# Combining the experts' rows by diagonal products on TensorE, and the second combining stage joined to the block behind it

## The chip, the cores and the metric

The kernel runs on one core of one Trainium2 chip. TensorE (PE) multiplies, VectorE (DVE), ScalarE (ACT) and GpSimd (POOL) do the elementwise work, and SyncE (SP) issues nearly all DMAs. The metric is the device time of one execution in microseconds (us), as the median of several.

## The reference, cut to what matters

512 tokens of width 1024 go through a first block of two layers and then a second block of two layers, all in fp32. In the first block each layer is a mixer (windowed attention, then latent attention), a layer norm, a routed expert stage and a second layer norm:

```
h = layer_norm(alpha * h + mixer(h), ln_g[i, 0], ln_b[i, 0])
y = hier_moe(h, ...)        # each token: the sum of 2 of 32 experts, each times a weight
h = layer_norm(alpha * h + y, ln_g[i, 1], ln_b[i, 1])
```

The second block has no experts: in each layer `x + rms_norm(mixer(rms_norm(x)))` and the same around a gated feed-forward. Its mixer joins a 31-tap convolution, stick-breaking attention, retention and a short convolution.

## The kernel before

The residual `k.resid` stays in SBUF as four tiles of 128 tokens x 1024. The expert stage (`experts`) leaves `alpha * h` in it and each token's two expert rows, not yet weighted, in a DRAM tensor `y_dram`; the two weights of a token lie in SBUF (`weight[:, c, t]`). What comes behind it is called an opening here. There are two.

**First opening**, at the head of `latent_layer`. SP loads the rows of a tile (1 MB each, line 1394), gains and weight pieces. VectorE's `weigh(t)` adds the two weighted rows to the residual (lines 1783 and 1784, one pass each) and takes the statistics (430, 432); ScalarE makes the inverse root (`AfterMix.root`, 437 and 439); VectorE's `norm` does two passes (447, 450). TensorE transposes the tile (`turn_x`, 1448), ScalarE copies the transposed tile out of PSUM rounded to fp32r (`split_high`, 1628), and VectorE subtracts that copy to get the low part (`split_low`, 1790). Every product with a weight is three fp32r products of high and low parts (`split_matmul`, 226 to 228), so weights are split as well: `high(p)` on ScalarE (1646) and `low(p)` on VectorE (1799), which frees the `raw` buffer for the next load. Each engine's order is written out by hand at the end of its function: VectorE does `weigh` 0, 1, `norm` 0, `weigh` 2, `norm` 1, `low(0)`, and so on. TensorE begins `down_tile` with tiles 0 and 1 (the first half of the columns) and takes tiles 2 and 3 once they are split.

**Second opening**, `combine` and the head of `second_block`. `combine` is a stage of its own: VectorE sums, takes statistics and normalizes all four tiles (1255 to 1270), ScalarE takes square roots (1285), GpSimd clears the semaphores of retired stages. A stage ends with a barrier of all engines, `close` adds another one with 12 more clears. Then `second_block` starts: SP loads the first two weight pieces, a gain and 22 small parameter rows; TensorE transposes the parameters (2381), ScalarE keeps them (2623). The RMS norm of a tile is ScalarE's square with a sum (2445), VectorE's scale-and-add-epsilon (2661), ScalarE's root (2432), VectorE's reciprocal and pass (2663, 2674). Then transpose (2092), high (2450) and low (2678) parts as above. `in_halves` runs four units on tiles 0 and 1, turning tile 3 behind its third, and then four on tiles 2 and 3. The same `finish`/`root`/`inverse_root` serve every norm of the block.

**Mixer of the second block** (`mixer` in each engine's function, once a layer). TensorE alternates projections (`project(u)`, 24 products of 512 columns) with attention and retention. Near its end: `ret_last(1)` makes scores, `decayed(1, 2)` on VectorE (2724) weights them, `ret_mix(1)` (2196) multiplies them with the values; `project(24)`, the statistics product (2279), which waits for the convolution's 62 taps (2701). VectorE's order there is `taps(6)`, `decayed(1, 0)`, `decayed(1, 1)`, `low(l, 11)`, `decayed(1, 2)`, `taps(8)`, `low(l, 12)`.

Of the kernel before, what the change touches and what calls it, by code (L numbers as in the profile page):

```python
# [20 lines left out]
P = 128  # L21
SEQ = 512
D = 1024
# [96 lines left out]
class Stage:  # L120
# [12 lines left out]
    def close(self):  # L133
        with self.nc.Block() as block:
            @block.gpsimd
            def _(pool):
                for s in self.sems:
                    pool.sem_clear(s)
        self.ctx.close()
        self.sem_ctx.close()  # L140

# [29 lines left out]
class Core:  # L171
# [16 lines left out]
    def clear_stale(self, eng):  # L188

        for st in self.stale:  # L190
            for s in st.sems:
                eng.sem_clear(s)

# [207 lines left out]
class AfterMix:  # L401
# [25 lines left out]
    def stats_of(self, k, dve, t):  # L427

        for half in range(2):
            dve.bn_stats(self.stats[:, t, half, :], k.resid[:, t, half * 512:(half + 1) * 512]).then_inc(self.counted, 1)  # L430
        dve.wait_ge(self.counted, 2 * t + 2)
        dve.bn_aggr(self.mv[:, t, :], self.stats[:, t, :, :]).then_inc(self.var_ready, 1)
# [8 lines left out]
    def norm(self, k, dve, t):  # L441

        x = k.resid[:, t, :]
# [3 lines left out]
        dve.scalar_tensor_tensor(x, x, self.mv[:, t, 0:1], self.gain[:, :], ALU.subtract, ALU.mult).then_inc(self.gained, 1)  # L447
# [4 lines left out]
    def turn(self, k, pe, rt, t):  # L452
# [4 lines left out]
        for j in range(ND):  # L457
            ins = pe.transpose(k.ps[:, 4 + j // 4, (j % 4) * P:(j % 4 + 1) * P], k.resid[:, t, j * P:(j + 1) * P], k.ident)
            if j % 4 == 3:
                ins.then_inc(rt.turned, 1)  # L460

# [763 lines left out]
def combine(k, layer, r):  # L1225

    st = Stage(k.nc, f"comb{layer}")
    gain, shift, warm = st.sb("gain", [P, D]), st.sb("shift", [P, D]), st.sb("warm", [P, 1])
    stats, mv, sd, rs = st.sb("stats", [P, NT, 2, 6]), st.sb("mv", [P, NT, 2]), st.sb("sd", [P, NT]), st.sb("rs", [P, NT])
    y_in = [st.sem(f"y{i}") for i in range(NT)]  # L1230
    gain_in, var_ready, sd_ready, summed, counted, gained, shifted, chain = (
        st.sem(n) for n in ("gain_in", "var", "sd", "summed", "counted", "gained", "shifted", "chain"))
    rows = k.ring[:, 0:4, :].rearrange("p s (c d) -> p s c d", c=2)
    y_rows = r.y_dram.rearrange("(c t p h) d -> t p c (h d)", c=TOPK, p=P, h=2)
    with k.nc.Block() as block:
        @block.sync
        def _(sp):
            for t in range(NT):
                sp.dma_start(rows[:, t], y_rows[t]).then_inc(y_in[t], 16)
                if t == 0:  # L1240
                    sp.dma_start(gain[:, :], k.a["ln_g"][layer, 1:2, :].to_broadcast([P, D])).then_inc(gain_in, 16)
                    sp.dma_start(shift[:, :], k.a["ln_b"][layer, 1:2, :].to_broadcast([P, D])).then_inc(gain_in, 16)

        @block.gpsimd
        def _(pool):
            k.clear_stale(pool)

        @block.vector
        def _(dve):
            link = Link(dve, chain)  # L1250

            def weigh(t):
                x = k.resid[:, t, :]
                dve.wait_ge(y_in[t], 16)
                link(dve.scalar_tensor_tensor(x, rows[:, t, 0, :], r.weight[:, 0, t:t + 1], x, ALU.mult, ALU.add))
                dve.scalar_tensor_tensor(x, rows[:, t, 1, :], r.weight[:, 1, t:t + 1], x, ALU.mult, ALU.add).then_inc(summed, 1)
                dve.wait_ge(summed, t + 1)
                for h in range(2):
                    dve.bn_stats(stats[:, t, h, :], x[:, h * 512:(h + 1) * 512]).then_inc(counted, 1)
                dve.wait_ge(counted, 2 * t + 2)  # L1260
                link(dve.bn_aggr(mv[:, t, :], stats[:, t, :, :]))
                dve.tensor_scalar(sd[:, t:t + 1], mv[:, t, 1:2], LN_EPS, None, ALU.add).then_inc(var_ready, 1)

            def finish(t):
                x = k.resid[:, t, :]
                dve.wait_ge(sd_ready, t + 1)
                dve.scalar_tensor_tensor(x, x, mv[:, t, 0:1], gain[:, :], ALU.subtract, ALU.mult).then_inc(gained, 1)
                link(dve.reciprocal(rs[:, t:t + 1], sd[:, t:t + 1]))
                dve.wait_ge(gained, t + 1)
                dve.scalar_tensor_tensor(x, x, rs[:, t:t + 1], shift[:, :], ALU.mult, ALU.add).then_inc(shifted, 1)  # L1270

            weigh(0)
            dve.wait_ge(gain_in, 32)
            for t in range(NT):
                if t + 1 < NT:
                    weigh(t + 1)
                finish(t)
            dve.wait_ge(shifted, NT)

        @block.scalar  # L1280
        def _(act):
            act.activation(warm[:, :], k.cst[:, C_ONE:C_ONE + 1], ACT.Sqrt)
            for t in range(NT):
                act.wait_ge(var_ready, t + 1)
                act.activation(sd[:, t:t + 1], sd[:, t:t + 1], ACT.Sqrt).then_inc(sd_ready, 1)
    k.free_stale()
    st.close()


LAT_UNITS = [(n, g) for n in range(NT) for g in range(4)]  # L1290

# [1613 lines left out]
```

## Time and profile before

| what | before |
| --- | --- |
| median of 3 runs (lowest, highest) | 2867.61 us (2865.9, 2874.51) |
| the profiled execution, its span | 2867.99 us, 2866.2 us |
| PE, PEld busy | 2492.6 us (87%), 1851.9 us (65%) |
| DVE, ACT, POOL busy | 1104.7 us (39%), 768.2 us (27%), 159.5 us (6%) |
| mean granted TensorE clock | 0.942 |
| 754 to 802: first opening | PE transposes from 772.0, products from 789.69 |
| 1576.7 to 1651: second opening | combining until 1610.8, products from 1636.57 |

The span runs from the first to the last instruction, and all starts are counted from its beginning. PE is the matmuls, PEld the weight loads beside them. An fp32 product counts as two instructions, an fp32r product as one. "Idle before <- releaser" is how long the engine stood still ahead of a group, and what ended that. The granted clock is a share of full speed: 1.00 is 2.4 GHz, 0.50 is 1.2 GHz.

### The profile page before, as it was taken

The numbers are of one execution on the slowest core, as the hardware profiler recorded it, in microseconds if no ns is written. First come the engines' busy times: TensorE is split into PE (matmuls) and PEld (weight loads), VectorE is DVE, ScalarE is ACT, GpSimd is POOL, SyncE is SP. The second block draws the span as 40 slices with busy tenths as digits, with TensorE's granted clock in tenths as the row PEclk, the third lists the DMA queues.
The fourth block names the chain that finished last, engine by engine and source line by source line (L and its number), as shares of the span: only waits on it lengthen the run. The fifth ranks groups of instructions, "written<-read, shape, count | busy, mean of one in ns | idle before, by whom it ended". The sixth has DMA issues, their size and how long they took to land. (4 is left out here: it accounts for less than half of the span.)

```text
span 2866.2 us, 36705 instructions
## 1 busy us (share of the span) xinstructions
PE 2492.6 (87%) x14450; PEld 1851.9 (65%) x14450; DVE 1104.7 (39%) x1653; ACT 768.2 (27%) x1219; POOL 159.5 (6%) x279
## 2 busy tenths in 40 slices
PE   8895998878388968987887299999999999999998
PEld 7574565544266655654544287688888876888887
DVE  3754111000444551110000565655551565655632
ACT  2430110000134510101000243444341452533331
POOL 0000111111000001111111000000000000000000
PEclk9997999999798979999999599999999999999999
DMA  5228999999612078999997421312332222223331
GB/s 153 59 81 330 407 405 409 411 408 402 218 70 74 8 285 342 405 404 406 408 409 291 143 96 59 118 59 88 103 118 102 82 68 80 74 89 102 98 123 52
DMA packets 174814, 576.38 MB, mean 201 GB/s; under 512 B 20496, under 2 KB 104016, under 8 KB 125042
## 3 DMA queue, kind: packets, MB, share of 16 engines
q1 hardware_dynamic: 164146, 558.07, 51.3%
q0 software_dynamic: 10560, 16.81, 1.8%
q8 instruction: 76, 1.25, 0.2%
q14 instruction: 32, 0.26, 0.0%
HBM read 569.56 MB, written 23.07 MB: 207 GB/s over the span
## 5 line engine op out<-in xcount | busy, mean ns | idle before, releaser
L1158 PE MATMUL ps<-first_weights,moe_xsT 128*64 128x256 f32 x2688 | 312.8, 381 | 50.1 <-DMA first_weights<-in_moe_w_up 32.1
L226 PE MATMUL ps<-l_h_hi,l_w_hi 128*128 128x512 f32 x896 | 353.1, 394 | 0.0
L227 PE MATMUL ps<-l_h_lo,l_w_hi 128*128 128x512 f32 x896 | 349.0, 389 | 0.0
L228 PE MATMUL ps<-l_h_hi,l_w_lo 128*128 128x512 f32 x896 | 349.0, 389 | 0.0
L1214 DVE TENSOR_TENSOR moe_hid<-moe_silu,ps 128x256 f32<-128x256 f32 x64 | 26.9, 421 | 796.2 <-PE ps L1158 796.2
L1158 PEld LDWEIGHTS ps<-first_weights,moe_xsT 128*64 128x64 f32 x2688 | 223.8, 137 | 148.8 <-issue 99.6
L2656 DVE TENSOR_TENSOR l_w_lo<-l_raw,l_w_hi 128x2048 fp32r<-128x2048 f32 x76 | 174.0, 2291 | 293.2 <-ACT l_w_hi L2427 293.2
L1195 ACT ACTIVATE moe_ys<-ps 128x512 f32<-128x512 f32 x64 | 38.2, 597 | 687.2 <-PE ps L1176 687.2
L1176 PE MATMUL ps<-first_weights,moe_hidT 128*64 128x512 f32 x672 | 178.9, 680 | 38.6 <-DVE moe_hidT L1216 38.6
L2427 ACT ACTIVATE l_w_hi<-l_raw 128x2048 fp32r<-128x2048 f32 x76 | 145.2, 1914 | 187.1 <-PE ps L228 176.0
L226 PEld LDWEIGHTS ps<-l_h_hi,l_w_hi 128*128 128x128 f32 x896 | 168.4, 188 | 37.7 <-issue 3.0
L1158 PE MATMUL ps<-first_ring,moe_xsT 128*64 128x256 f32 x1408 | 168.6, 391 | 26.3 <-DMA first_ring<-in_moe_w_up 14.0
L227 PEld LDWEIGHTS ps<-l_h_lo,l_w_hi 128*128 128x128 f32 x896 | 168.4, 188 | 35.4 <-issue 1.4
L228 PEld LDWEIGHTS ps<-l_h_hi,l_w_lo 128*128 128x128 f32 x896 | 168.3, 188 | 35.4
L1158 PEld LDWEIGHTS ps<-first_ring,moe_xsT 128*64 128x64 f32 x1408 | 119.6, 141 | 79.4 <-issue 52.8
L1176 PEld LDWEIGHTS ps<-first_weights,moe_hidT 128*64 128x64 f32 x672 | 60.6, 153 | 127.9 <-issue 127.9
L1176 PE MATMUL ps<-first_ring,moe_hidT 128*64 128x512 f32 x352 | 88.9, 650 | 20.1 <-DVE moe_hidT L1216 20.1
L1142 PEld LDWEIGHTS ps<-cst,moe_xs 64*128 64x128 f32 x528 | 68.9, 215 | 45.9 <-issue 24.6
L1142 PE MATMUL ps<-cst,moe_xs 64*128 64x64 f32 x528 | 78.0, 289 | 20.8 <-DMA moe_xs<-r_x,moe_take 20.8
L1130 POOL DMA_INDIRECT r_y<-moe_ys,moe_put x64 | 65.4, 1022 | 298.6 <-ACT moe_ys L1195 298.6
L2701 DVE SCALAR_TENSOR_TENSOR l_gate<-l_glu,l_par,l_gate 128x512 f32<-128x512 f32 x120 | 81.0, 744 | 0.1
L1192 ACT ACTIVATE moe_silu<-ps 128x256 f32<-128x256 f32 x64 | 24.5, 383 | 204.8 <-PE ps L1158 204.8
(545 smaller groups left out, 4279.6 us busy)
## 6 DMA issues: line engine op xcount, KB each, us to landing
first_weights<-in_moe_w_up SPq DMA_DIRECT2D x84, 1024.0 KB, 29.0
first_weights<-in_moe_w_down SPq DMA_DIRECT2D x84, 1024.0 KB, 28.8
first_weights<-in_moe_w_gate SPq DMA_DIRECT2D x84, 1024.0 KB, 28.3
first_ring<-in_moe_w_gate SPq DMA_DIRECT2D x44, 1024.0 KB, 28.1
first_ring<-in_moe_w_up SPq DMA_DIRECT2D x44, 1024.0 KB, 29.1
first_ring<-in_moe_w_down SPq DMA_DIRECT2D x44, 1024.0 KB, 28.9
l_raw<-in_ffn_up SPq DMA_DIRECT2D x44, 1024.0 KB, 5.1
l_raw<-in_w_in SPq DMA_DIRECT2D x24, 1024.0 KB, 5.3
```

The source lines that it names most:

```text
L226: pe.matmul(out, stationary[0], moving[0], start=first, stop=False)
L227: pe.matmul(out, stationary[0], moving[1], start=False, stop=False)
L228: return pe.matmul(out, stationary[1], moving[0], start=False, stop=last)
L1130: pool.indirect_dma_start(out=r.y_dram, out_offset=bass.IndirectOffsetOnAxis(ap=put[:, 0:1], axis=0), in_=ys[:, :], in_offset=None, bounds ...
L1142: ins = pe.transpose(k.ps[:, 0, j * SLOTS:(j + 1) * SLOTS], row_of_tile[:, j // 4, j % 4, :], k.cst[0:SLOTS, C_ID:C_ID + SLOTS])
L1158: ins = pe.matmul(k.ps[64 * h:64 * h + 64, 2 + m, 0:256], xsT[:, j, :], weights.gate_up[s][m][:, j, 256 * h:256 * h + 256], start=j == 0, ...
L1176: ins = pe.matmul(k.ps[64 * h:64 * h + 64, 4, :], hidT[:, j % 2, 64 * (j // 2):64 * (j // 2) + 64], weights.down[s][:, j, 512 * h:512 * h ...
L1195: act.activation(ys[:, :], k.ps[:, 4, :], ACT.Copy).then_inc(ys_kept, 1)
L1214: dve.tensor_tensor(hid[:, :], silu[:, :], k.ps[:, 3, 0:256], ALU.mult).then_inc(hid_kept, 1)
L2427: act.activation(ring[n][0], raw[:, m % 2, :], ACT.Copy).then_inc(hi_made, 1)
L2656: dve.tensor_tensor(lo, raw[:, m % 2, :], hi.bitcast(F32), ALU.subtract).then_inc(lo_made, 1)
L2701: ins = dve.scalar_tensor_tensor(acc, glu[:, i, c:c + SEQ], par[:, l, 2, 2 * c + i:2 * c + i + 1], acc, ALU.mult, ALU.add)
```

## The change

Both openings sum on TensorE. A new class `Collect` loads the rows, makes for each tile and choice a 128x128 diagonal matrix of the weights on ScalarE, and adds in PSUM: identity x residual, then diagonal x rows, all in fp32. A tile takes two banks, so the four tiles fill all eight. Statistics and the first normalizing pass read PSUM.

```
+    def diagonals(self, k, act):
+        for t in range(NT):
+            for c in range(TOPK):
+                ins = act.activation(self.diag[:, c, t, :], k.ident, ACT.Copy, scale=self.before.weight[:, c, t:t + 1])
+        ins.then_inc(self.spread, 1)
+
+    def own(self, k, pe):
+        for t in range(NT):
+            for half in range(2):
+                pe.matmul(k.ps[:, 2 * t + half, :], k.ident, k.resid[:, t, half * 512:(half + 1) * 512], start=True, stop=False)
+
+    def add(self, k, pe, t):
+        pe.wait_ge(self.spread, 1)
+        pe.wait_ge(self.y_in[t], 16)
+        for half in range(2):
+            for c in range(TOPK):
+                ins = pe.matmul(k.ps[:, 2 * t + half, :], self.diag[:, c, t, :], self.rows[t][:, c, half * 512:(half + 1) * 512], start=False, stop=c == TOPK - 1)
+        ins.then_inc(self.collected, 1)
```

`norm` is cut in two: `centre(k, dve, t, src)` does subtract mean and times gain from `src` (PSUM) into the residual, and `finish` does the second pass.

First opening, per engine:

```
 TensorE
+            cl.own(k, pe)
+            cl.add(k, pe, 0)
+            cl.add(k, pe, 1)
             turn_x(0)
+            cl.add(k, pe, 2)
             turn_x(1)
+            cl.add(k, pe, 3)
 GpSimd, behind its clears
+            for p in range(2):
+                pool.wait_ge(hi_made, p + 1)
+                pool.tensor_tensor(whole(p, 1), raw[:, p, :], whole(p, 0).bitcast(F32), ALU.subtract).then_inc(lo_made, 1)
 ScalarE
+            cl.diagonals(k, act)
             cm.root(act, 0)
             high(0)
             cm.root(act, 1)
             split_high(0)
+            high(1)
+            split_high(1)
             cm.root(act, 2)
-            split_high(1)
-            high(1)
+            split_high(2)
             cm.root(act, 3)
-            split_high(2)
             split_high(3)
 VectorE (weigh, norm, low(0) and low(1) go)
+            stats(0)                       # waits for collected, statistics from PSUM
+            cm.centre(k, dve, 0, tile_banks(0))
+            cm.finish(k, dve, 0)
+            stats(1)
+            cm.centre(k, dve, 1, tile_banks(1))
+            cm.finish(k, dve, 1)
             split_low(0)
+            stats(2)
+            cm.centre(k, dve, 2, tile_banks(2))
             split_low(1)
+            cm.finish(k, dve, 2)
+            stats(3)
+            cm.centre(k, dve, 3, tile_banks(3))
             split_low(2)
+            cm.finish(k, dve, 3)
             split_low(3)
+            dve.wait_ge(lo_made, 2)
```

Second opening: `combine` and `close` go. `second_block` begins with one short block, `sweep`, in which SP issues the loads of rows and gains while GpSimd, VectorE and ScalarE clear a third of the old semaphores each; its barrier stands ahead of the rest.

```
 TensorE
+            cl.own(k, pe)
+            for t in range(NT):
+                cl.add(k, pe, t)
             turn(opening, 0)
             turn(opening, 1)
-            turn(opening, 2)
-            pe.wait_ge(par_kept, 2)
             for l in range(DEPTH):
-                in_halves(l, ...)          # turned tile 3 behind its third unit
+                in_halves(l, ...)          # l == 0: tile 2 behind the second unit, tile 3 behind the fourth
+                if l == 0:
+                    turn_parameters()
 ScalarE
+            cl.diagonals(k, act)
+            deviation(0)                   # Sqrt of the variance + epsilon
+            finish(opening, 0, None)       # square with sum, root
+            deviation(1)
+            split_high(opening, 0)
+            finish(opening, 1, None)
             high(0, 0)
+            deviation(2)
+            split_high(opening, 1)
             high(0, 1)
             finish(opening, 2, None)
+            deviation(3)
+            split_high(opening, 2)
             finish(opening, 3, None)
             split_high(opening, 3)
 VectorE (normed: reciprocal and cm.finish; finish: the RMS norm's pass; stats: statistics and centre)
+            stats(0)
+            normed(0)
+            stats(1)
+            finish(opening, 0)
+            normed(1)
+            split_low(opening, 0)
+            stats(2)
+            finish(opening, 1)
+            split_low(opening, 1)
+            normed(2)
+            stats(3)
+            finish(opening, 2)
+            split_low(opening, 2)
+            normed(3)
+            finish(opening, 3)
+            split_low(opening, 3)
+            dve.wait_ge(lo_made, 2)
```

GpSimd makes the low parts of the first two weight pieces here too. The parameters are kept by ScalarE behind `high(l, 3)` in layer 0; TensorE waits for that ahead of `project(6)`, VectorE ahead of the taps, and the load of the rotation tables waits for the parameters' transposes.

In every norm of the second block the scale and epsilon move into ScalarE's root, and VectorE's instruction goes; ScalarE's `finish` of tile t waits for tile t-2's sum where there is no transpose:

```
-                act.wait_ge(g.biased, v)
-                act.activation(sd[...], sd[...], ACT.Sqrt).then_inc(g.rooted, 1)
+                act.wait_ge(g.squared, v)
+                act.activation(sd[...], ss[...], ACT.Sqrt, scale=1.0 / D, bias=eps[:, 0:1]).then_inc(g.rooted, 1)
```

In the mixer's VectorE order, in both layers:

```
                 decayed(1, 0)
                 decayed(1, 1)
+                decayed(1, 2)
                 low(l, 11)
-                decayed(1, 2)
                 taps(8)
```

## Rows read from the trace of the kernel before

**Rows 1.** The expert rows' tile and DMA issues, first opening
```profile
L1394 SPq DMA_DIRECT2D lat_rows<-r_y x4: 388/607/3402, 753.9 to 760.0; - x4
...
DMA to landing us min/median/max: 4.9/11.6/14.2
...
lat_raw<-in_b_w_down SPq DMA_DIRECT2D x2, 1024.0 KB, 14.1
```

**Rows 2.** Table by stretches: start:end length, busy time (instructions) of each engine, clock, DMA
```profile
772.00:789.60 17.60, 3.93 (x16) 3.13 (x16) 17.18 (x18) 4.84 (x7) 0.00 (x0) 0.50 0.45 111
789.60:794.50 4.90, 4.81 (x22) 4.81 (x23) 4.71 (x4) 0.00 (x0) 0.00 (x0) 0.50 0.02 3
1576.70:1612.60 35.90, 0.00 (x0) 0.00 (x0) 26.90 (x36) 2.30 (x6) 0.00 (x0) 0.50 0.38 147
1636.50:1641.00 4.50, 4.50 (x23) 4.50 (x23) 2.53 (x3) 1.02 (x1) 0.00 (x0) 0.50 0.00 0
1799.30:1803.80 4.50, 4.50 (x17) 1.75 (x17) 4.50 (x8) 0.00 (x0) 0.00 (x0) 0.50 0.00 0
```

**Rows 3.** Timeline, first opening: start, us, engine, line, operation, count [idle before]
```profile
768.18 1.91 ACT L1646 ACTIVATE lat_d_hi<-lat_raw 128x2048 fp32r<-128x2048 f32 x1 [4.54 <-DMA lat_raw<-in_b_w_down]
...
774.00 1.02 ACT L1628 ACTIVATE lat_x_hi<-ps 128x1024 fp32r<-128x1024 f32 x1 [3.49 <-PE ps L1448]
...
780.68 1.22 DVE L1790 TENSOR_TENSOR lat_x_lo<-ps,lat_x_hi 128x1024 fp32r<-128x1024 f32 x1
...
789.69 0.58 PE L226 MATMUL ps<-lat_x_hi,lat_d_hi 128*128 128x256 f32 x1 [9.11 <-DVE lat_x_lo L1790]
...
794.80 1.03 PE L1448 MATMUL ps<-cst,resid 128*128 128x128 f32 x8
...
801.95 0.38 PE L226 MATMUL ps<-lat_x_hi,lat_d_hi 128*128 128x256 f32 x1 [2.37 <-DVE lat_x_lo L1790]
```

**Rows 4.** Timeline, second opening
```profile
1578.15 1.78 SPq L1239 DMA_DIRECT2D first_ring<-r_y  x3
...
1584.20 1.29 DVE L1259 BATCH_NORM_STATS2 comb_stats<-resid 128x6 f32<-128x512 f32 x2
...
1609.55 1.28 DVE L1270 SCALAR_TENSOR_TENSOR resid<-resid,comb_rs,comb_shift 128x1024 f32<-128x1024 f32 x1
...
1612.66 1.00 SPq L2036 DMA_DIRECT2D l_raw<-in_w_in  x2
...
1624.51 1.04 ACT L2445 ACTIVATE l_end_xn<-resid 128x1024 f32<-128x1024 f32 x1
...
1636.57 0.56 PE L226 MATMUL ps<-l_h_hi,l_first_hi 128*128 128x256 f32 x1
...
1648.05 0.36 PE L226 MATMUL ps<-l_h_hi,l_first_hi 128*128 128x256 f32 x1
```

**Rows 5.** Timeline, end of the mixer in layer 0; last row: layer 1
```profile
1793.89 1.91 ACT L2427 ACTIVATE l_w_hi<-l_raw 128x2048 fp32r<-128x2048 f32 x1 [6.31 <-PE ps L228]
...
1795.83 2.29 DVE L2656 TENSOR_TENSOR l_w_lo<-l_raw,l_w_hi 128x2048 fp32r<-128x2048 f32 x1 [7.70 <-ACT l_w_hi L2427]
...
1799.10 5.38 DVE L2701 SCALAR_TENSOR_TENSOR l_gate<-l_glu,l_par,l_gate 128x512 f32<-128x512 f32 x8
...
1799.24 4.53 PE L2196 MATMUL ps<-l_wr,l_vt 128*64 128x512 f32 x16 [5.39 <-DVE l_wr L2724]
...
1809.81 1.88 PE L2279 MATMUL ps<-l_gate,cst 128*128 128x512 f32 x4
...
2425.16 1.88 PE L2279 MATMUL ps<-l_gate,cst 128*128 128x512 f32 x4
```

**Rows 6.** fp32 products (timeline) and a VectorE pass reading PSUM (its tile)
```profile
1705.21 4.50 PE L2187 MATMUL ps<-l_ln,cst 128*128 128x512 f32 x20
...
L2669 DVE SCALAR_TENSOR_TENSOR l_end_xn<-ps,l_rs,l_end_gain x8: 1282/1284/1286, 2227.4 to 2860.6; 128x1024 f32<-128x1024 f32 x8
```

**Rows 7.** Timeline, end of layer 0: the instruction ahead of a root
```profile
2231.27 0.15 DVE L2661 TENSOR_SCALAR l_sd<-l_ss 128x1 f32<-128x1 f32 x1 [1.29 <-ACT l_end_xn L2445]
```

More of the change, by code:

```diff
@@ L192, in clear_stale, with sweep, _ @@
                 eng.sem_clear(s)
+    def sweep(self, loads):
+        sems = [s for st in self.stale for s in st.sems]
+        third = -(-len(sems) // 3)
+        with self.nc.Block() as block:
+            @block.sync
+            def _(sp):
+                loads(sp)
+            @block.gpsimd
+            def _(pool):
+                for s in sems[:third]:
+                    pool.sem_clear(s)
+            @block.vector
+            def _(dve):
+                for s in sems[third:2 * third]:
+                    dve.sem_clear(s)
+            @block.scalar
+            def _(act):
+                for s in sems[2 * third:]:
+                    act.sem_clear(s)
+        self.free_stale()
     def free_stale(self):
@@ L441, in norm, with centre @@
     def norm(self, k, dve, t):
-        x = k.resid[:, t, :]
+        self.centre(k, dve, t, k.resid[:, t, :])
+        self.finish(k, dve, t)
+    def centre(self, k, dve, t, src):
         if t == 0:
@@ L1222, in experts @@
     st.retire(k)
[L1225 to L1287, printed above, removed]
@@ L1778, in _, with stats @@
             link = Link(dve, chain)
[L1780 to L1786 removed]
+            def stats(t):
+                dve.wait_ge(cl.collected, t + 1)
+                cm.stats_of_sum(k, dve, t)
             def split_low(t):
@@ L1988, in second_block, with first_loads @@
     rows = plan.put("rows", 32, [P, DEPTH, 3, P])
+    cl = Collect(st, plan, (36, 44, 68, 76), 24, before)
+    cm = AfterMix(st, plan, "c", 0, 84)
+    def first_loads(sp):
+        cl.load(sp, 0)
+        cm.load_gains(k, sp, DEPTH - 1, 1)
+        for t in range(1, NT):
+            cl.load(sp, t)
+    k.sweep(first_loads)
     in_w = [(w.hi[:, n, :], w.lo[:, n, :]) for n in range(2)]
@@ L2116, in up_unit, with in_halves @@
                 return ins
-            def in_halves(l, g, one, piece, made):
+            def in_halves(l, g, one, piece, made, turns=((), (), (3,), ())):
                 pe.wait_ge(g.h_lo, 2)
@@ L2124, in in_halves @@
                     one(q, slice(0, 2 * P))
-                    if q == 2:
-                        turn(g, 3)
+                    for t in turns[q]:
+                        turn(g, t)
                 pe.wait_ge(g.h_lo, NT)
```

153 lines of the change are left out of this document (74 added, 79 removed).

## The prediction

> **What bounds the kernel now.** I read the page first: TensorE is busy most of the span and the chain of waits runs through it. So I looked in the table by stretches for those where TensorE stands still, and in the timeline for what it waits for there. Three places matter.
>
> First opening: the second layer's block starts at 753.9 (the first load of expert rows) [rows 1]. VectorE combines, normalizes and splits four tiles, busy 17.18 of 17.60 us, while TensorE's granted clock is 0.50, its lower level (1.2 GHz) [rows 2]. TensorE's first product starts at 789.69, the second half of the tokens at 801.95 [rows 3].
>
> Second opening: the combining block takes 1576.7 to 1612.6, with no TensorE instruction [rows 2]; the second block starts its loads at 1612.66, its first product runs at 1636.57. The last quarter of the first two tiles' work starts at 1648.05 [rows 4] and has 24 products; at the upper clock they take some 0.12 us each, about half of the 4.81 us that 22 of this shape take at the lower [rows 2]. So the second half of the tokens begins at 1650.9.
>
> Mixer, once in each layer: TensorE stands 5.39 us before the last retention product because VectorE does a 2.29 us low part before the last decay products; that low part itself had waited 7.70 us for ScalarE, idle [rows 5]. The ScalarE copy it waited for starts at 1793.89, when TensorE's preceding projection ends. The product then takes 4.53 us [rows 5], at a granted clock of 0.50 [rows 2], so after idling it runs at half the upper clock, 2.3 us lost.
>
> Elsewhere in the second block TensorE is hardly ever idle, so what these places give stays given: weights, copies and low parts are all released by products or by each other, none by the clock on the wall.
>
> **Prices of what is added.** TensorE gets 24 fp32 products of 128x512 in each opening (8 own, 16 weighted). The nearest row holds ten fp32 products, 2560 columns in all, in 4.50 us [rows 6]; less 0.17 for the last one's drain that is 1.69 ns a column, 0.87 us for 512. At 1.2 GHz it is 1.74. Two sustained stretches turn to 2.4 GHz after 4.9 and 4.5 us [rows 2], so a run that begins cold costs 2.25 us more: own takes 8 x 0.87 + 2.25 = 9.2 us, each tile's add 3.5 us. Eight diagonals on ScalarE are 1024 columns, the width of a 1.04 us square [rows 4]; with seven more starts an estimated 2.5 us, hidden behind own. VectorE loses two weighted adds of 1.28 a tile and keeps statistics (1.29 + 0.21) and two passes of 1.28; that centre now reads PSUM is free, since the same operation from PSUM takes 1.284 [rows 6]. Transpose of a tile: 1.03 at 2.4 GHz, twice that at 1.2; high part 1.02, low part 1.22 [rows 3].
>
> GpSimd gets two subtractions of 128x2048, which VectorE does in 2.29 [rows 5]. No row shows one on GpSimd. Low end 2.29; as high end I take four times that, 9.2; between them twice, 4.6, an estimate. The Trainium skill (GPSIMD Engine Reference, 3.1 Elementwise — side-by-side cycle accounting) gives 4497 ns against 2293 ns for this size; VectorE's row agrees with the second figure, no row here has the first, and with it the sum would be the same.
>
> **First opening.** Own runs from 753.9 to 763.2. The first expert tile lands 4.9 us after 753.9, the last no later than 14.2 after 760.0, at 774.2 [rows 1]. Adds end at 766.7 and 770.2. Tile 0: statistics to 768.3, centre 769.6, finish 770.9 (ScalarE's root lies beside centre); transposed to 772.1. Tile 1: statistics 772.4, centre 773.7, finish 775.0; add 2 has TensorE until 775.6, transposed to 776.7; add 3 to 780.2. The second weight piece is now copied before tile 1's high part. The two pieces have a median landing of 14.1 us [rows 1] and the first lands 12.2 after its issue at 756.0 (ScalarE starts on it at 768.18 [rows 3]), so the second, issued at 760.6, lands 16.0 later, 776.6; copy 778.5, high part 779.5, low part 780.8. First product at 780.9 against 789.69: 8.8 us. GpSimd's first subtraction (770.8 to 775.4) has 5.5 us to spare. Then 24 products at 2.4 GHz (2.9), transpose 784.9, high 786.0, low 787.2 (finish 2, statistics 3 and centre 3 lie before it, to 784.9), finish 3 788.5, transpose 789.6, high and low 791.8. Second half at 791.9 against 801.95: **10.0 us**. Before, the first half ran at 1.2 GHz; that is part of it.
>
> **Second opening.** The new block issues its loads in 3.2 us (the last three take 1.78 from 1578.15 [rows 4]); 17 clears on each of three engines stay under that, since 12 of them with all barriers fit between the last pass, 1610.8, and 1612.66. With 0.9 for barriers TensorE starts at 1580.8. Own to 1590.0, adds to 1593.5, 1597.0, 1600.5, 1603.9; the tiles have landed before each. VectorE: statistics 0 1595.1, centre 1596.4, finish 1597.9; tile 1 statistics and centre 1600.7; round 0 (ScalarE's square and root ended 1599.5) 1602.2; finish 1 1603.7. TensorE turns tile 0 at 1603.9 to 1604.9, high 1606.0, low 1607.3; statistics and centre 2 to 1610.1; round 1 to 1611.6; turned cold 1613.7, high 1614.8, low 1616.1. ScalarE's first weight copy ends 1609.4, GpSimd's subtraction 1614.0. First product at 1616.2 against 1636.57: 20.4 us. But then VectorE is late again: 48 products half cold, 7.7 us, to 1623.9; turn 2 1624.9, low 1627.2; finish 3 1628.7; square and root 1630.2; round 3 1631.7; turn 1632.7; low 1635.0. Second half at 1635.1 against 1650.9: 15.8. The parameter transposes now stand behind it, 0.9 us, and the tables' load behind them, with projections in front of its use: **14.9 us**.
>
> **Mixer.** The scores for the last decay products were long ready, since VectorE stood idle before 1795.83. Now they run there, and the last retention product starts at 1793.9 and takes half of 4.53, the projection 5.5 (in layer 0 it ended at 1809.81, 6.0 after the product, the first 0.6 at the low clock): 1801.7. What is late next is the convolution: low part to 1798.1, eight taps 5.38 [rows 5], to 1803.5. The statistics product starts then against 1809.81, 6.3 us. In layer 1 it starts at 2425.16, and the taps end 5.6 us before that. TensorE takes the lead again behind: VectorE's next low part moves forward with ScalarE's copy by more than that. Together **11.9 us**.
>
> **Roots.** One VectorE instruction of 0.15 us with its two hand-overs goes from each chain [rows 7]: 0.3 at the turn from layer 0 to 1, 0.3 at the last tile, 0.3 at the feed-forwards: **0.9 us**. The new wait on tile t-2's sum is met 8 us early.
>
> **Sum.** The profiled execution took 2867.99 us (span 2866.2, 1.8 around it), 0.4 above the median 2867.61. 2867.99 - 10.0 - 14.9 - 11.9 - 0.9 = 2830.3; against the median 2829.9. I forecast **2830**.
>
> **Rivals.**
> A: GpSimd's subtractions and VectorE's passes get in each other's way. As a mechanism here: a VectorE pass with both inputs in SBUF (finish, the rounds) that comes during a GpSimd subtraction waits for its end. Finish 1 at 773.7 waits to 775.4, finish 2 a little: 1.1 us by the second half. Round 1 at 1610.3 waits to 1614.0 and round 2 to the end of the second subtraction: second half 1638.6 instead of 1635.1, 3.5. Together 4.6: 2834.5. For it: both have work at once in both openings. Against: no row of before shows the two together. The Trainium skill (SBUF — State Buffer, Who interferes with whom) says just this: a VectorE instruction with two SBUF inputs contends with a GpSimd one that reads SBUF, and the later one blocks fully; no run yet shows it.
> B: GpSimd needs 9.2 us. Its end passes the first opening's start (780.0) not at all and the second's (1618.6 for 1616.2; the second piece later by 4): some 4 us, with A's waits up to 12: 2834 to 2842.
> C: the moved decay products give nothing, the chain behind (taps, low parts, ScalarE's copies) being the bound: 2867.6 - 25.8 = 2842. For it: 1.8 us of the idle time is already convolution. Against: that chain is released by ScalarE's copy behind the projection, which moves forward by more than the statistics product does.
> D, the other side: the clock. If fp32 products with their gaps don't bring TensorE up and it stays at 1.2 GHz through both openings, 24 products cost 41.8 us. First opening: adds and two turns end at 799.6, second half at 816.2 against 801.95 and runs 4.5 longer: 18.7 lost. Second: adds to 1622.6, first product 1635.8, second half 1662.6 against 1650.9 and 9 longer, 0.9 and as much again for parameters: 22.5 lost. With the other terms kept, 2867.6 + 41.2 - 12.8 = 2896. It decides once about two thirds of the products run cold. For it: 0.50 throughout the openings, and fp32 products at 1.2 GHz in 1799.24's row. Against: those came after idling, and both sustained starts rose within 5 us.
>
> **Chances.** Forecast 0.50, A 0.28, B 0.07, C 0.10, D 0.03, something else 0.02. Quicker barriers and hand-overs can give some 6 us more, and the mixer what the convolution holds back, 1.8 in each layer: 2821. C with A ends at 2846: range 2821 to 2846. This measurement tells 0.3% (8.6 us) from no change: faster 0.95, same 0.02, slower 0.03.
>
> **What would show it.** First product 28 us after the first row load instead of 35.8, and about 40 us after the second's instead of 59.8; granted clock 1.00 from about 5 us into own; 0.87 us a product; the 5.39 us waits gone and some 1.8 us before the statistics product; GpSimd's subtractions near 4.6 us, and VectorE passes of 1.28 us grown long beside them if A holds. Wrong would be an opening that ends with TensorE's adds instead of VectorE, or a mixer as long as before.

## The result, and the profile after

The changed kernel takes 2843.64 us (median of 4 runs, 2842.8 to 2846.85) against 2868.07 of the kernel before on the same chip (4 runs): the ratio is 0.9913, 95% interval 0.9896 to 0.9931. The forecast was 2830, the range 2821 to 2846. The gain is 24.4 us where 38 were forecast, so the time lies inside the range, but 13.6 us of the gain are missing, and the rest of the study is about them.

The head of the page and the granted clock row of the changed kernel:

```profile
span 2841.4 us, 36857 instructions
PE 2533.8 (89%) x14546; PEld 1870.4 (66%) x14546; DVE 1078.5 (38%) x1597; ACT 776.1 (27%) x1234; POOL 179.0 (6%) x284
PEclk9996999999998978999999799999999999999999
```

TensorE is busy 41 us longer than before, in the main by its added products (48 of about 0.86 us), in a span that is 25 us shorter; GpSimd has 20 us more, its four subtractions.

First opening, the changed kernel's timeline (start, us, engine, line, operation, count, idle before). The rows answer to [rows 3]; the first load of expert rows stands at 755.17, 1.3 us later than before with nothing changed ahead of it (over all traces of this study it stands between 752.85 and 755.76).

```profile
755.21 9.28 PE L512 MATMUL ps<-resid,cst 128*128 128x512 f32 x16 [10.13 <-PEq L1148]
...
772.08 4.60 POOL L1436 TENSOR_TENSOR lat_d_lo<-lat_raw,lat_d_hi 128x2048 fp32r<-128x2048 f32 x1 [16.74 <-ACT lat_d_hi L1646]
...
775.17 2.59 DVE L474 SCALAR_TENSOR_TENSOR resid<-resid,lat_crs,lat_cshift 128x1024 f32<-128x1024 f32 x1
...
779.59 4.56 POOL L1436 TENSOR_TENSOR lat_d_lo<-lat_raw,lat_d_hi 128x2048 fp32r<-128x2048 f32 x1 [2.92 <-ACT lat_d_hi L1646]
...
782.71 2.52 DVE L474 SCALAR_TENSOR_TENSOR resid<-resid,lat_crs,lat_cshift 128x1024 f32<-128x1024 f32 x1
782.84 0.39 PE L242 MATMUL ps<-lat_x_hi,lat_d_hi 128*128 128x256 f32 x1 [0.50 <-DVE lat_x_lo L1787]
...
801.35 0.34 SPq L1406 DMA_DIRECT2D lat_tables<-in_k_ropeb  x1
```

Own took 9.28 us (forecast 9.2) and the first product came 27.7 us after the first load (35.8 before, forecast gain 8.8, here 8.1). But two finishing passes of VectorE, 1.28 us elsewhere, took 2.59 and 2.52 us, each while GpSimd subtracted.

Second opening, same columns; it answers to [rows 4]:

```profile
1570.15 0.39 SPq L499 DMA_DIRECT2D l_rows<-r_y  x1
...
1602.53 4.49 POOL L2095 TENSOR_TENSOR l_first_lo<-l_raw,l_first_hi 128x2048 fp32r<-128x2048 f32 x1 [28.29 <-ACT l_first_hi L2452]
...
1603.35 4.76 DVE L2708 SCALAR_TENSOR_TENSOR l_end_xn<-resid,l_rs,l_end_gain 128x1024 f32<-128x1024 f32 x1
...
1608.16 1.97 PE L2109 MATMUL ps<-cst,l_end_xn 128*128 128x128 f32 x8 [10.01 <-DVE l_end_xn L2708]
...
1612.50 0.58 PE L242 MATMUL ps<-l_h_hi,l_first_hi 128*128 128x256 f32 x1 [2.37 <-DVE l_h_lo L2712]
...
1613.06 5.22 POOL L2095 TENSOR_TENSOR l_first_lo<-l_raw,l_first_hi 128x2048 fp32r<-128x2048 f32 x1 [6.04 <-ACT l_first_hi L2452]
...
1616.71 2.65 DVE L2708 SCALAR_TENSOR_TENSOR l_end_xn<-resid,l_rs,l_end_gain 128x1024 f32<-128x1024 f32 x1
...
1627.92 1.09 PE L2109 MATMUL ps<-cst,l_end_xn 128*128 128x128 f32 x8 [1.11 <-DVE l_end_xn L2708]
...
1631.38 0.58 PE L242 MATMUL ps<-l_h_hi,l_first_hi 128*128 128x256 f32 x1 [2.37 <-DVE l_h_lo L2712]
...
1646.45 0.35 SPq L2072 DMA_DIRECT2D l_tables<-in_k_roper  x1
```

The pass of 4.76 us began 0.8 us behind the subtraction and could only work once that ended at 1607.02; TensorE and ScalarE stood behind it. First product 42.4 us after the first load (59.8 before): 17.5 gained, 20.4 forecast.

The mixer came as forecast. The last retention product and the statistics product of layer 0, then the latter in layer 1 [rows 5]:

```profile
1777.69 2.37 PE L2213 MATMUL ps<-l_wr,l_vt 128*64 128x512 f32 x16
1787.44 1.98 PE L2299 MATMUL ps<-l_gate,cst 128*128 128x512 f32 x4 [1.72 <-DVEq L2820]
...
2398.63 1.98 PE L2299 MATMUL ps<-l_gate,cst 128*128 128x512 f32 x4 [1.72 <-DVEq L2820]
```

No wait before the product, 2.37 us instead of 4.53, and 1.72 us of waiting for the convolution behind it (forecast 1.8).

The granted clock of TensorE is the other finding. The changed kernel's table by stretches (start:end length, busy time (instructions) of PE, PEld, DVE, ACT and POOL, clock, DMA share, GB/s): the start of the second half of the tokens in both openings, then the beginning of the down projections of both layers.

```profile
793.90:799.00 5.10, 5.10 (x31) 5.10 (x32) 3.17 (x3) 1.31 (x2) 0.00 (x0) 0.68 0.01 2
1631.30:1636.30 5.00, 4.92 (x23) 4.92 (x24) 4.36 (x3) 2.37 (x2) 0.00 (x0) 0.50 0.01 3
2107.00:2113.00 6.00, 6.00 (x20) 4.72 (x20) 4.80 (x6) 4.83 (x4) 0.00 (x0) 0.72 0.13 55
2719.00:2725.00 6.00, 6.00 (x21) 4.74 (x21) 4.80 (x5) 4.32 (x4) 0.00 (x0) 0.73 0.08 9
```

and the same places of the kernel before:

```profile
802.00:807.00 5.00, 5.00 (x42) 5.00 (x43) 3.13 (x3) 1.27 (x2) 0.00 (x0) 1.00 0.00 0
1650.00:1655.00 5.00, 5.00 (x44) 5.00 (x43) 4.35 (x3) 4.84 (x4) 0.00 (x0) 1.00 0.00 0
2127.00:2133.00 6.00, 4.22 (x19) 3.49 (x19) 4.72 (x8) 3.51 (x4) 0.00 (x0) 1.00 0.50 172
2739.00:2751.00 12.00, 10.22 (x45) 8.11 (x44) 10.69 (x11) 5.87 (x6) 0.00 (x0) 1.00 0.26 89
```

Before, the waits in front of the first opening's second half (2.37 us) and of the down projections (1.78 us) cost only themselves, and in the second opening TensorE did not wait there at all. Now a wait stands in front of all four (2.37 us in each opening), and each is followed by a stretch at 1.2 GHz. A mean clock of 0.72 over 6 us is (1 - 0.72) x 6 = 1.7 us lost. The wait ahead of the down projection is the same to the hundredth in both kernels, first the kernel before, then the changed one:

```profile
2128.79 0.50 PE L226 MATMUL ps<-l_w_hi,l_act_hi 128*128 128x512 f32 x1 [1.78 <-DVE l_conv L2831]
```

```profile
2106.50 0.50 PE L242 MATMUL ps<-l_w_hi,l_act_hi 128*128 128x512 f32 x1 [1.78 <-DVE l_conv L2866]
```

### The profile page after: what moved, and what is told of

It is laid out like the page before. It is cut to its first block and busy times, and to the rows that moved or that the text cites. A ratio compares the mean times of both kernels' runs of the same rounds, so it can differ in the third digit from the quotient of the medians.

```text
span 2841.4 us, 36857 instructions
## 1 busy us (share of the span) xinstructions
PE 2533.8 (89%) x14546; PEld 1870.4 (66%) x14546; DVE 1078.5 (38%) x1597; ACT 776.1 (27%) x1234; POOL 179.0 (6%) x284
## 5 line engine op out<-in xcount | busy, mean ns | idle before, releaser
L242 PEld LDWEIGHTS ps<-l_h_hi,l_w_hi 128*128 128x128 f32 x896 | 168.2, 188 | 37.4 <-issue 2.9
L242 PE MATMUL ps<-l_w_hi,l_act_hi 128*128 128x512 f32 x192 | 77.0, 401 | 3.6 <-DVE l_conv L2866 3.6
```

The costliest lines, as they stand in the source:

```text
L242: pe.matmul(out, stationary[0], moving[0], start=first, stop=False)
```

## The experiments

Two theories came out of this reading. The **port theory** is rival A: a VectorE pass with both inputs in SBUF waits for GpSimd's subtraction, as if both needed one port of SBUF that only one of them can hold. "Port" and "lock" are names for this waiting; what the traces show is the waiting. The **clock theory**: short waits of TensorE that cost nothing before now cost the granted clock. Each expectation is on record as written before its run.

The openings are measured from the first load of expert rows to the issue of the rotation tables' load, which waits until TensorE has got a set way into the work behind the opening. That is one profiled execution for each kernel; time is the median, d the difference to the changed kernel.

```
kernel               time     d      ratio to before (95%)    1st    2nd opening
before               2868.07                                  54.1   86.0
changed              2843.64         0.9913 (0.9896, 0.9931)  46.2   76.3
e1_mixer             2858.17  +14.5  0.9969 (0.9958, 0.9980)
e2_no_subtraction    2839.11   -4.5  0.9903 (0.9887, 0.9918)  45.0   73.5
e3_fill              2838.82   -4.8  0.9901 (0.9886, 0.9917)  45.5   74.4
e4_order             2832.63  -11.0  0.9880 (0.9865, 0.9895)  46.9   66.0
e5_openings          2851.72   +8.1  0.9941 (0.9927, 0.9954)  46.9   77.4
e6_low_on_vector     2843.85   +0.2  0.9919 (0.9905, 0.9932)  48.6   75.6
e7_order_both        2829.25  -14.4  0.9862 (0.9846, 0.9877)  42.9   66.0
e8_order_fill        2826.18  -17.5  0.9860 (0.9845, 0.9876)  42.7   65.7
e9_fill_down         2838.80   -4.8  0.9902 (0.9885, 0.9920)  47.1   76.2
e10_subtract_twice   2845.43   +1.8  0.9922 (0.9906, 0.9937)  47.0   76.3
```

The kernel before took 2868.1, 2868.2 and 2867.2 beside the three groups of experiments, so the times can be set side by side within some 2 us; single runs of one kernel spread over 2 to 12. The changed kernel, e5, e9 and e10 have the same work on the path of both openings: their means, 46.8 and 76.5, are what the others are compared with below. These four spread over 0.9 and 1.2 us, so a difference in an opening of less than about 1 us says nothing.

**e1_mixer.** In the kernel before:

```
                 decayed(1, 1)
+                decayed(1, 2)
                 low(l, 11)
-                decayed(1, 2)
```

> The kernel before with one thing of the change: in the mixer VectorE does the last decay products ahead of its low part. My theory (TensorE leads, the freed 5.4 us wait and the cold product are worth 6.3 us in layer 0 and 5.6 in layer 1): 2867.8 - 11.9 = 2856, and the trace shows the last retention product with no wait before it and some 1.8 us of idle before the statistics product. Rival C (taps, low parts and copies are the bound behind it): 2867. Clock theory, from the trace of the changed kernel (short idle times of TensorE now and then cost the granted clock, with no rule that the change sets): up to 1.7 us may be lost again in each down projection, 2859; then the stretch behind the 1.8 us wait for the convolution shows a granted clock under 1.00.

2858.17 us, 10.0 under before. In place it is the forecast: the product takes 2.37 us with no wait, and 1.72 us of idle stand before the statistics product. In layer 0 the down projection keeps its clock, in layer 1 it doesn't:

```profile
2116.00:2128.00 12.00, 10.22 (x46) 8.13 (x45) 10.27 (x11) 6.38 (x7) 0.00 (x0) 1.00 0.24 87
2731.00:2737.00 6.00, 5.88 (x19) 4.70 (x20) 4.76 (x6) 4.84 (x4) 0.00 (x0) 0.72 0.26 104
```

11.7 us (6.2 and 5.5, as the changed kernel's trace has them) less one loss of 1.7 is the 10.0 measured; that they meet so closely is in part luck, since e1's runs spread over 3.9 us and only the profiled one shows its clock. Rival C is out.

**e2_no_subtraction.** In both openings of the changed kernel (the low parts are zeros that GpSimd wrote earlier, so that part of the product adds nothing):

```
-                pool.tensor_tensor(lo, raw[:, n, :], hi.bitcast(F32), ALU.subtract).then_inc(lo_made, 1)
+                pool.sem_inc(lo_made, 1)
```

> The changed kernel, with GpSimd's four subtractions left out (the low parts of the first two weight pieces of each of the two openings are zero, filled by GpSimd before; its hand-over to TensorE stays behind ScalarE's copy). Port theory (a VectorE pass with both inputs in SBUF waits for GpSimd's subtraction to end): the passes of 2.59, 2.52, 4.76 and 2.65 us fall to 1.28; first opening 1 to 2 us shorter, second 3 to 4: 2843.6 - 5 = 2838.6. Rival (those passes are long for another reason, as a late operand from ScalarE or the DMA writes into SBUF): they stay long, 2843.6. Second rival (what waits behind them is TensorE's clock, not VectorE): passes fall to 1.28, the time stays within 1 us.

2839.11 us, 4.5 faster. The pass that took 4.76 us in the changed kernel, in e2:

```profile
1601.69 1.28 DVE L2714 SCALAR_TENSOR_TENSOR l_end_xn<-resid,l_rs,l_end_gain 128x1024 f32<-128x1024 f32 x1
```

All four passes are at 1.28. The first opening is 1.8 us shorter, the second 3.1. The loads into SBUF are the same in e2, so they were not what held the passes. The port theory stands, with its size. With this loss gone the prediction's walk through the queues holds nearly to the us: counted from the first row load, its first products are at 27.0 and 39.5 us and its second halves at 38.0 and 58.4; e2 has them at 26.4 and 39.3, and at 37.4 and 58.3 (the changed kernel at 27.7 and 42.4, and at 38.7 and 61.2).

**e3_fill.** In the changed kernel; the first lines in both openings (bank 3 in the first, 4 in the second; there behind a wait for the third low part), the second in each down projection. Cut to the products and the wait that they precede:

```
+                for n in range(5):
+                    pe.matmul(k.ps[:, 4, 0:2 * P], k.ident, k.resid[:, 0, 0:2 * P], start=True, stop=True)
                 pe.wait_ge(g.h_lo, NT)
...
+                for n in range(4):
+                    pe.matmul(k.ps[:, 4, 0:2 * P], zeros[:, :], k.resid[:, 0, 0:2 * P], start=False, stop=False)
                 pe.wait_ge(x.convolved, 4 * STEPS)
```

> The changed kernel, with products added that nobody reads: five fp32 128x256 (0.43 us each) into a free bank while TensorE waits for the last low part of each opening, and four with a zero stationary before the wait for the convolution in each down projection. Clock theory (a wait of 1.8 to 2.4 us there drops the granted clock to 0.50 for 2 to 4 us): the second halves start at clock 1.00, 1.5 us gained in the first opening, 2.2 in the second, 1.7 in each down projection: 2843.6 - 7 = 2836.5. Rival (the clock falls whatever TensorE does there, or the fill delays the start by as much as it saves): 2843 to 2845.

2838.82 us, 4.8 faster with more instructions. The four places in e3's table by stretches:

```profile
792.00:800.00 8.00, 7.79 (x57) 7.18 (x56) 4.45 (x4) 3.65 (x4) 0.00 (x0) 1.00 0.01 3
1630.00:1638.00 8.00, 7.79 (x57) 7.18 (x56) 5.64 (x3) 4.63 (x3) 0.00 (x0) 1.00 0.00 0
2102.00:2114.00 12.00, 11.96 (x53) 9.65 (x53) 10.68 (x11) 4.84 (x4) 0.00 (x0) 1.00 0.30 100
2718.00:2726.00 8.00, 8.00 (x37) 6.64 (x36) 4.86 (x3) 3.26 (x2) 0.00 (x0) 1.00 0.39 134
```

1.00 in all four. The openings are 1.3 and 2.1 us shorter by the traces. With TensorE busy in the wait the clock stays up; the rival, that it falls whatever TensorE does there, is out. Idle time alone doesn't decide it, since the same waits cost no clock in the kernel before. The traces of the four places add up to 6.8 us, the times show 4.8.

**e9_fill_down.** Only the lines in the down projections.

> The changed kernel with only the down projections' fill: four fp32 128x256 products with a zero stationary before TensorE's wait for the convolution. Clock theory (in the changed kernel, though not in the kernel before, this wait of 1.8 us costs the granted clock, 1.7 us in each layer): both down projections run at 1.00, 2843.6 - 3.4 = 2840.2. Rival (the mixer moves forward and something else in that phase is late): 2843 to 2845 and the clock, if it stays up, gives nothing.

2838.80 us: 4.8 faster, more than the 3.4 expected and as much as e3 with all four; the runs of each spread over 6 to 8 us, so e3 and e9 can't be told apart by their times. What the fills in the openings are worth is therefore shown by e3's trace alone, and not by a time. e9's down projections:

```profile
2102.00:2110.00 8.00, 7.96 (x36) 6.35 (x35) 6.68 (x9) 4.61 (x4) 0.00 (x0) 1.00 0.41 131
2714.00:2722.00 8.00, 7.96 (x36) 6.28 (x35) 6.72 (x8) 4.85 (x4) 0.00 (x0) 1.00 0.31 123
```

**e5_openings.** The changed kernel with the mixer's order of before (e1's diff, reversed).

> The changed kernel with the mixer's order of before (VectorE's low part ahead of the last decay products): what the two openings and the roots are worth by themselves. If the parts add up, the 10.0 us that the mixer gave alone are lost again: 2843.6 + 10 = 2853.6, that is 14 to 15 us under before. Rival (the parts hinder each other; the openings alone give the 24.9 us of the prediction, and the mixer's shift costs them later): 2843 to 2847.

2851.72 us, 8.1 slower: the mixer's move is worth 8.1 us on top of the openings, not 11.7 (e5's runs spread over 7.6 us). e5 has the cold retention product again, and its down projections keep their clock with no fill:

```profile
1784.35 4.36 PE L2213 MATMUL ps<-l_wr,l_vt 128*64 128x512 f32 x16 [5.38 <-DVE l_wr L2758]
```

```profile
2107.00:2122.00 15.00, 13.22 (x59) 10.61 (x58) 12.18 (x11) 6.92 (x7) 0.00 (x0) 1.00 0.31 98
2728.00:2740.00 12.00, 12.00 (x53) 9.95 (x54) 7.01 (x6) 6.03 (x5) 0.00 (x0) 1.00 0.52 192
```

11.7 - 2 x 1.7 = 8.3. The expectation's first figure was 1.9 too high. That fits its taking e1's 10.0, in which only one down projection lost its clock, though 1.9 us is also no more than two such times can differ by. Over all traces, one profiled execution of each kernel: with the mixer's product cold, at 1.2 GHz (before, e5), none of 4 down projections lost its clock; with it at 2.4 GHz and no fill (changed, e1, e2, e4, e6, e7, e10) 13 of 14 did; with the fill (e3, e8, e9) none of 6. That the one decides the other is a count, not a mechanism. Nothing near the wait tells the cases apart: in the traces of before, changed, e1, e5 and e10 TensorE is busy without a gap at clock 1.00 for 28 us ahead of it, and the wait is 1.78 us each time. Why a stretch 330 us earlier should matter stays open.

**e6_low_on_vector.** The changed kernel without GpSimd's subtractions; VectorE has `low(0)` and `low(1)` behind the finishing pass of tile 1 and the low part of tile 1 (first opening), `low(0, 0)` behind statistics and centre 2 and `low(0, 1)` behind the low part of tile 1 (second).

> The changed kernel with GpSimd's four subtractions given back to VectorE (2.29 us each, as VectorE's low parts before), right behind the high parts. Port theory: first opening 4.6 longer for VectorE less the 1.3 and 1.2 us of waits that go, some 2 us; second opening 2.3 in place of a wait of 3.5 and 2.3 in place of one of 1.4, about nothing: 2843.6 + 2 = 2845.6, so that moving them off VectorE was worth next to nothing. Rival (GpSimd takes them off the path for what they cost on VectorE): 4.6 in each opening, 2852.8.

2843.85 us, the same as the changed kernel. First opening 1.8 longer, second 0.9 shorter. As placed in the change, moving 9.2 us of VectorE's work to GpSimd was worth nothing that these runs can tell, since VectorE then waited 7.4 us in its four long passes.

**e10_subtract_twice.** GpSimd subtracts the first piece of the second opening twice.

```
+                if n == 0:
+                    pool.tensor_tensor(lo, raw[:, n, :], hi.bitcast(F32), ALU.subtract).then_inc(cleared, 1)
+                    pool.wait_ge(cleared, 3)
                 pool.tensor_tensor(lo, raw[:, n, :], hi.bitcast(F32), ALU.subtract).then_inc(lo_made, 1)
```

> The changed kernel with GpSimd's subtraction of the first weight piece of the second opening done twice in a row (the same result, 4.5 us more for GpSimd). If the port is held over both: VectorE's pass of 4.76 us grows to 9.2 and the opening by 4.5, 2848. If the port changes hands between two instructions: VectorE's pass slips in at the end of the first, 4.76 as before, the second subtraction starts 1.1 to 1.3 later, ends about where the first product starts, and costs 0.2 to 1 us: 2844.3. Without a lock (only the piece's landing counts): the second subtraction ends 0.9 us before the first product, nothing, 2843.6, and VectorE's pass is what it was or overlaps the second.

2845.43 us, 1.8 above the changed kernel and inside its spread; the second opening is unchanged, 76.3. The time alone decides little. The second theory of the three is what the trace has:

```profile
1601.58 4.49 POOL L2096 TENSOR_TENSOR l_first_lo<-l_raw,l_first_hi 128x2048 fp32r<-128x2048 f32 x1 [28.34 <-ACT l_first_hi L2455]
1602.39 4.76 DVE L2711 SCALAR_TENSOR_TENSOR l_end_xn<-resid,l_rs,l_end_gain 128x1024 f32<-128x1024 f32 x1
1606.15 5.38 POOL L2098 TENSOR_TENSOR l_first_lo<-l_raw,l_first_hi 128x2048 fp32r<-128x2048 f32 x1
1607.21 1.97 PE L2112 MATMUL ps<-cst,l_end_xn 128*128 128x128 f32 x8 [10.01 <-DVE l_end_xn L2711]
```

VectorE works between the two, and the second subtraction waits for VectorE in turn: 5.38 instead of 4.49. It ends at 1611.53, and the first product follows at 1611.68, as that theory had it. So the waiting is by instruction and goes both ways.

**e4_order.** The changed kernel, the same instructions in another order. The second opening (VectorE, then ScalarE, then TensorE's `turns`; cut: ScalarE's `high(0, 1)` and its deviations 2 and 3 also come earlier):

```
             stats(1)
+            stats(2)
             finish(opening, 0)
             normed(1)
             split_low(opening, 0)
-            stats(2)
             finish(opening, 1)
+            stats(3)
             split_low(opening, 1)
             normed(2)
-            stats(3)
-            finish(opening, 2)
-            split_low(opening, 2)
             normed(3)
+            finish(opening, 2)
             finish(opening, 3)
+            split_low(opening, 2)
...
             deviation(0)
+            high(0, 0)
             finish(opening, 0, None)
...
-  ((), (2,), (), (3,))
+  ((2,), (3,), (), ())
```

In the first, `split_low(0)` stands ahead of finish 1, and statistics and centre 3 ahead of finish 2 and 3.

> The changed kernel with another order of the same instructions in the openings: VectorE's statistics and centre passes (one input in PSUM) stand where GpSimd subtracts, ScalarE makes the high part of the first weight piece of the second opening some 8 us earlier, and TensorE turns tiles 2 and 3 of the second opening after its first and second quarter instead of second and fourth. Port theory with the order of waits read from the trace: passes of 1.28 us throughout; second opening: first product about 5 us earlier, second half 7.7 us earlier (53.5 us after the first row load instead of 61.2) and without a cold restart (2); first opening 1.5 to 3 us: 2843.6 - 11.5 = 2832. Rival (what binds is TensorE's cold product train and the landing of the weights, the lock hides behind them): under 3 us, 2841.

2832.63 us, 11.0 faster. The second opening is 10.5 us shorter, the first not at all, where 1.5 to 3 were expected (VectorE waited there for ScalarE's fourth root, as e7's expectation says). e4's timeline beside GpSimd's first subtraction of the second opening:

```profile
1592.43 4.53 POOL L2095 TENSOR_TENSOR l_first_lo<-l_raw,l_first_hi 128x2048 fp32r<-128x2048 f32 x1 [17.89 <-ACT l_first_hi L2452]
...
1593.48 1.28 DVE L467 SCALAR_TENSOR_TENSOR resid<-ps,l_cmv,l_cgain 128x1024 f32<-128x1024 f32 x1
1594.68 1.29 DVE L446 BATCH_NORM_STATS2 l_cstats<-ps 128x6 f32<-128x512 f32 x2
...
1596.24 1.28 DVE L467 SCALAR_TENSOR_TENSOR resid<-ps,l_cmv,l_cgain 128x1024 f32<-128x1024 f32 x1
1597.63 1.28 DVE L2708 SCALAR_TENSOR_TENSOR l_end_xn<-resid,l_rs,l_end_gain 128x1024 f32<-128x1024 f32 x1
```

Statistics and centre read PSUM and run beside the subtraction at their usual 1.28: only passes with both inputs in SBUF are held up.

That is the smaller part of the 10.5. With no subtraction at all e2's second opening takes 73.5 us, and e4's, with both subtractions, 66.0. So the waits for the port account for 3.1 at most, and the other 7.4 come from the rest of the order: in e2 TensorE still stands 1.11 and 2.37 us ahead of the second half and restarts cold there (2.1 by e3), while in e4, with tiles 2 and 3 turned earlier, it doesn't stand still:

```profile
1614.00:1640.00 26.00, 26.00 (x203) 25.04 (x202) 7.70 (x5) 9.72 (x15) 0.25 (x2) 1.00 0.10 32
```

How much each of the moves gives was not measured.

**e7_order_both.** e4 with `cm.root(act, 3)` ahead of `split_high(2)`, and `turn_x(3)` ahead of `down_tile(1)`, where `turn_x(2)` already was.

> The reordered kernel (e4_order), whose first opening was 0.7 us longer than the changed kernel's because VectorE waited 2.66 us for ScalarE's fourth root, which stood behind the high part of tile 2. Here ScalarE makes that root first, and TensorE turns tiles 2 and 3 before the second quarter of the first products. If VectorE's order is what binds: second half 37.3 us after the first row load instead of 39.4, and with no wait before it, so at clock 1.00 (1.7 more): 2832.6 - 3.8 = 2828.8. Rival (TensorE's products, now behind the turns, bind): second half no earlier than 39 us, 2831 to 2833.

2829.25 us, 3.4 under e4. The first opening is 42.9, 4.0 shorter than e4's; it has no wait before the second half (8.00 of 8 us busy at clock 1.00), so the rival is out. The second row is the first products of the second opening, which begin cold:

```profile
790.00:798.00 8.00, 8.00 (x64) 7.74 (x63) 3.68 (x4) 1.82 (x3) 0.00 (x0) 1.00 0.03 8
1600.00:1612.00 12.00, 9.35 (x52) 8.95 (x53) 10.06 (x15) 5.63 (x10) 4.52 (x1) 0.61 0.28 89
```

**e8_order_fill.** e7 with the fills listed in its expectation.

> e7_order_both with products that nobody reads in TensorE's waits: four fp32 128x256 before the turn of tile 2 in the first opening, eight and five behind the turns of tiles 0 and 1 in the second, four with a zero stationary before the wait for the convolution in each down projection. Clock theory: in the second opening the turn of tile 1 takes 1.04 instead of 1.97 us and the first products run at 1.00 from the start (2.3 more), each down projection keeps its clock (1.7): 6.7 us under e7, 2822. Rival (the clock falls by something else than TensorE's idle time, or the fills delay what they precede): 2827 to 2830.

2826.18 us (2822.33 to 2832.06), 3.1 under e7, not 6.7. The down projections are at clock 1.00 again, which by e9's expectation is worth 3.4 us; it isn't measured apart here. The second opening has clock 1.00 where e7 has 0.61, and yet is only 0.3 shorter: the first product comes 0.7 us earlier, and then TensorE waits for VectorE:

```profile
1594.00:1612.00 18.00, 14.47 (x106) 13.15 (x105) 13.73 (x18) 8.96 (x15) 4.54 (x1) 1.00 0.18 60
```

```profile
1599.93 0.39 PE L242 MATMUL ps<-l_h_hi,l_first_hi 128*128 128x256 f32 x1 [0.69 <-DVE l_h_lo L2724]
1605.37 1.09 PE L2113 MATMUL ps<-cst,l_end_xn 128*128 128x128 f32 x8 [2.30 <-DVE l_end_xn L2720]
```

It has the lowest median, 17.5 us under the changed kernel's, though it can't be told from e7 by its interval.

## Why the prediction was right in direction, and a third of its gain did not come

Point by point, with the prediction's own terms:

- **Prices** were right: own 9.28 (9.2), diagonals 2.44 (2.5), GpSimd's subtraction 4.49 to 4.62 (4.6, taken as twice VectorE's). Rival B is out by that, and rival D by the clock: own took 9.28 us with its cold start and the next eight products 7.03, not 13.9. A small slip stands in the list of signs, which gives 28 us to the first product where the schedule gives 27.0.
- **First opening**, 10.0 forecast: the four traces with this work give 54.1 - 46.8 = 7.3. The port takes 1.8 (e2), the cold start of the second half 1.3 (e3); together 10.4. The walk through the engines' queues was right (see e2), and the forecast left both losses out, the first of them as rival A.
- **Second opening**, 14.9: 86.0 - 76.5 = 9.5; the port takes 3.1 (e2), the cold start 2.1 (e3); together 14.7. Rival A had priced its waits at 1.1 and 3.5, 4.6 together, against the 4.9 of e2, by the mechanism that the runs bore out. The two engines' work overlaps in the prediction's own schedule (773.7 in 770.8 to 775.4; 1610.3 in 1609.4 to 1614.0), and the only thing against A was that no row of before showed the two together, which is no evidence that they don't meet. So 0.28 was too low a chance, and A's 2834.5 the better forecast. The runs show 2.59, 2.52, 4.76 and 2.65 us beside the subtraction, 1.28 without it (e2), and 1.28 for passes from PSUM beside it (e4). The Trainium skill (SBUF — State Buffer, Who interferes with whom) has it so: a VectorE instruction with two SBUF inputs contends with a GpSimd one that reads SBUF, one with at most one SBUF input, outside the two-port modes, does not. The trace agrees, by these numbers.
- **Mixer**, 11.9: 11.7 in place, but 8.1 measured by e5. **The step that failed** here is "TensorE is hardly ever idle, so what these places give stays given". It looked for waits that would grow. None did: the 1.78 us wait of the down projection stayed 1.78 us, but it now costs the clock as well, 1.7 us in each layer (the stretches at 0.72 in the changed kernel; e9 and e5 agree in time within their spread).
- **The clock in the openings** failed in the same way: the first opening's wait of 2.37 us was in [rows 3] with products at the full clock behind it, so it was carried over as a wait only. In the second opening the schedule makes TensorE stand both before and after the turn of tile 3, and puts a cold start there at nothing, though the prediction had a price for one, 2.25 us. In the changed kernel the 2.37 us before each second half is followed by a loss of 1.3 and 2.1 us.
- **Roots**, 0.9: not measured by themselves; too small for these runs. It isn't shown that they gave anything.

The account: 37.7 of the sum, less 4.9 (port), 3.4 (cold starts in the openings) and 3.4 (down projections) is 26.0, against 24.4 measured. The 1.6 left is smaller than the spread of single runs and isn't explained further. Added up from what was measured, the openings' 7.3 and 9.5 and the mixer's 8.1 are 24.9. That 2843.64 still lay in the range, near its upper end of 2846, is in part luck: that end was worked out for a mixer that gives nothing (C) together with A, and C did not happen; the clock losses, 6.8 us by the traces, took its place.

## What to carry to other kernels

When work moves to GpSimd, list VectorE's passes that have both inputs in SBUF and fall beside it; put the passes that read PSUM there instead. Here such waits cost 4.5 to 4.9 us (e2), as much as taking the work off VectorE had saved (from e6 to e2, 4.7). And set each engine's order by who is late next: the same instructions in another order gave 11 us, of which the port can account for 3.1. A wait of TensorE has two prices, its length and the clock behind it, and a trace in which the second is zero doesn't promise that it stays so: count waits of some 2 us ahead of dense products at 1.3 to 2.1 us each in the range, as they cost here, and fill them if a bank is free. After every queue's walk look once more at who is late next: fills in a place where VectorE was next gave 0.3 us of the 3.3 expected of them.

## What the runs showed of the hardware

- A VectorE pass with both inputs in SBUF and a GpSimd subtraction take turns, instruction by instruction, and either can be the one that waits: the subtraction took 4.49 us when VectorE's pass came behind it, and 5.22 and 5.38 when such a pass was running at its start (changed kernel, e10).
- The wait of 1.78 us ahead of the down projection left the granted clock at 1.00 in 5 cases (before, e5, e1's first) and was followed by a fall to 1.2 GHz in 13, at 1.7 us each. What decides between them is open.
- Products with a zero stationary that add into a bank in use kept the clock at 1.00 in 6 of 6 down projections (e3, e8, e9) and cost nothing that could be measured.
